# Two layers written out without a loop, with the splits of weights laid between tiles and row parts

## The reference

```python
for i in range(2):
    x = x + 0.5 * swiglu_ffn(rmsnorm_2(x, ffn1_norm[i]), ffn1_wi[i], ffn1_wo[i])
    u = rmsnorm_2(x, mix_norm[i])
    mq, mk, mv, mo, mi, mf, sq, sk, sv, ga, gb = jnp.split(u @ w_in[i], offsets, axis=-1)
    hA = rmsnorm_2(mlstm_chunkwise(mq, mk, mv, mi + b_igate[i], mf + b_fgate[i]), ml_out_norm[i])
    yA = (jax.nn.sigmoid(mo) * hA) @ w_a[i]
    hB = swa_sink_attention(sq, sk, sv, q_norm[i], k_norm[i], sinks[i], rel_bias)
    mixed = jax.nn.sigmoid(ga) * yA + jax.nn.sigmoid(gb) * (hB @ w_b[i])
    x = x + mixed @ w_out[i]
    x = x + 0.5 * swiglu_ffn(rmsnorm_2(x, ffn2_norm[i]), ffn2_wi[i], ffn2_wo[i])
    gate = jax.nn.sigmoid(rmsnorm_2(x, ple_norm[i]) @ w_ple_gate[i])
    x = x + gate * (p[i] @ w_ple[i])
```

## Time and profile before

| | us |
|---|---|
| median of three runs | 2400.02 |
| the profiled execution's own time | 2400.93 |
| its span | 2398.9 |
| TensorE matmul busy | 1921.8 (80%) |
| TensorE weight load busy | 1366.8 (57%) |
| VectorE busy | 969.2 (40%) |
| ScalarE busy | 696.0 (29%) |
| GpSimd busy | 40.6 (2%) |

### The profile page before, as it was taken

One profiled execution on the slowest core, in us unless ns is written; L12 is line 12 of the kernel. 1 busy time (PEld: TensorE's weight loads), 2 busy tenths in 40 slices (PEclk: granted clock), 3 DMA queues, 4 the chain that ended last, 5 costly groups with the idle time before them and its releaser, 6 DMA issues.

```text
span 2398.9 us, 34233 instructions
## 1 busy us (share of the span) xinstructions
PE 1921.8 (80%) x12667; PEld 1366.8 (57%) x12667; DVE 969.2 (40%) x1348; ACT 696.0 (29%) x963; POOL 40.6 (2%) x68
## 2 busy tenths in 40 slices
PE   6996655655555555565899999899989999989998
PEld 4774111211111111111799877799879988778997
DVE  3474000000000000000676576666656666666665
ACT  4331000000000000000444455444444444544443
POOL 0000000000000000000000000000000000000000
PEclk9997778778787778778999999999999999999999
DMA  9767999999999999999556553355535565344561
GB/s 370 251 241 331 429 428 429 428 428 429 428 428 428 428 428 428 428 428 410 181 199 217 163 157 123 122 176 196 189 107 182 186 203 176 124 136 150 171 208 55
DMA packets 174825, 660.85 MB, mean 275 GB/s; under 512 B 10053, under 2 KB 108142, under 8 KB 143734
## 3 DMA queue, kind: packets, MB, share of 16 engines
q1 hardware_dynamic: 171980, 654.12, 70.4%
q10 hardware_dynamic: 2376, 3.03, 0.6%
q0 software_dynamic: 352, 2.11, 0.2%
HBM read 656.60 MB, written 2.64 MB: 275 GB/s over the span
## 4 chain that ended last, share of the span: by engine, by line
issue 77%; PE 17%; DVE 3%; ACT 1%; POOL 1%; DMA 1%; POOLq 0%; ACTq 0%; DVEq 0%; PEldq 0%; PEld 0%
PE PS L1862 12%; PE PS L1577 2%; DVE units L205 1%; DVE arena L205 1%; DMA ring<-in_w_ada 1%; PE PS L1546 1%; ACT units L205 0%; POOL arena L604 0%; PE PS L1643 0%; PE PS L1661 0%; DVE hn L205 0%; POOLq L603 0%; POOLq L629 0%; DVE x L205 0%; DVE hT_split L205 0%
## 5 line engine op out<-in xcount | busy, mean ns | idle before, releaser
L205 DVE TENSOR_TENSOR units<-ring,units 128x1024 fp32r<-128x1024 f32 (+2 forms) x416 | 505.7, 1216 | 206.7 <-ACT units L205 172.1
L205 ACT ACTIVATE units<-ring 128x1024 fp32r<-128x1024 f32 (+2 forms) x416 | 438.0, 1053 | 482.7 <-PE PS L1862 447.4
L1862 PE MATMUL PS<-hT_split,units 128*128 128x256 f32 x4416 | 554.9, 286 | 10.0 <-DVE hT_split L205 8.4
L1862 PEld LDWEIGHTS PS<-hT_split,units 128*128 128x128 f32 x4416 | 547.8, 194 | 20.5 <-DVE hT_split L205 11.3
L205 DVE SCALAR_TENSOR_TENSOR arena<-arena,PS 128x512 f32<-128x512 f32 (+1 forms) x54 | 41.4, 767 | 802.5 <-ACT arena L205 513.1
L205 ACT ACTIVATE arena<-PS 32x256 f32<-32x256 f32 (+4 forms) x135 | 66.8, 495 | 945.9 <-PE PS L1832 310.7
L1862 PE MATMUL PS<-units,hT_split 128*128 128x512 f32 (+2 forms) x1248 | 294.2, 396 | 13.3 <-DVE hT_split L205 9.0
L1862 PEld LDWEIGHTS PS<-units,hT_split 128*128 128x128 f32 x1248 | 238.1, 195 | 61.3 <-DVE hT_split L205 9.8
L1862 PE MATMUL PS<-units,hid_split 128*128 128x512 f32 x1056 | 255.6, 392 | 0.0
L1862 PEld LDWEIGHTS PS<-units,hid_split 128*128 128x128 f32 x1056 | 192.8, 189 | 37.0 <-issue 0.9
L1824 PE MATMUL PS<-moe_ring,arena 128*32 128x512 f32 x768 | 124.5, 781 | 98.9 <-DMA moe_ring<-in_w_gate_e 55.8
(11 more groups left out here) (208 smaller groups left out, 1254.7 us busy)
## 6 DMA issues: line engine op xcount, KB each, us to landing
ring<-in_ffn_wi SPq DMA_DIRECT2D x88, 1024.0 KB, 5.4
ring<-in_w_gate_e SPq DMA_DIRECT2D x24, 2048.0 KB, 36.0
moe_ring<-in_w_up_e SPq DMA_DIRECT2D x24, 2048.0 KB, 36.4
ring<-in_w_down_e SPq DMA_DIRECT2D x24, 2048.0 KB, 35.6
moe_ring<-in_w_gate_e SPq DMA_DIRECT2D x24, 2048.0 KB, 36.7
ring<-in_w_up_e SPq DMA_DIRECT2D x24, 2048.0 KB, 36.5
moe_ring<-in_w_down_e SPq DMA_DIRECT2D x24, 2048.0 KB, 36.2
ring<-in_ffn_wo SPq DMA_DIRECT2D x44, 1024.0 KB, 4.9
```

The costliest lines, as they stand in the source:

```text
L205: return instruction(*args, **kwargs)
L1862: passes = [mm(out, lhs[i], rhs[j], start=start and i + j == 0, stop=stop and i == 1, **flags) for i, j in ((0, 0), (0, 1), (1, 0))]
```

## The change

The layer loops of all engines become Python loops: each engine's program holds both layers, and semaphore targets outside the FFN loops are constants. The FFN loops stay. The first units of layer 1's FFN1 are split inside layer 0's PLE stage, and the first square of `x` is taken there. Unit rests are laid between token tiles and between row parts. The first product of an FFN takes both its units part by part (`first_up`). The transposed parts of the mix stage lie in other banks, so that half of `ple_up` can go ahead of them. Squares and sums of queries and keys go ahead of the scans. ScalarE makes `a_split` ahead of `sw_exp(7)`.

```diff
-def turned_bank(name):
-    return 0 if name in ("mix", "ple") else 4
+def turned_bank(name, k):
+    return {"mix": (0, 1, 4, 5), "ple": (0, 1, 2, 3)}.get(name, (4, 5, 6, 7))[k % 4]
+ROOT_BANK = {"ffn1": 3, "mix": 0, "ffn2": 3}
...
-            with sp.Fori(0, LAYERS) as l:
+            for l in range(LAYERS):
...
-            for l in act.loop(LAYERS):
+            for l in range(LAYERS):
                 before = FIRST_UNITS + l * LAYER_UNITS
                 layer_fills = l * (LAYER_SLOTS // R * 16)
-                gate_up_hi(OFF_FFN1, 0, before, layer_fills)
+                if l == 0:
+                    gate_up_hi(OFF_FFN1, 0, before, layer_fills)
...
                     sw_copy(h)
+                    if h == 6:
+                        halves_hi(stage_units(OFF_WA, 2, 0, 2), D, before, layer_fills)
+                        act.wait_ge(S["branch_T"], 2 * l + 1)
+                        activation(a_split[:, 0, :, :].rearrange("p k n -> p (k n)"), two_banks(4), ACT.Copy).then_inc(
+                            S["branch_hi"], 1)
                     if h + 1 < SW_H:
                         sw_exp(h + 1)
...
                     if h == 6:
-                        halves_hi(stage_units(OFF_WA, 2, 0, 2), D, before, layer_fills)
-                        act.wait_ge(S["branch_T"], 2 * l + 1)
-                        activation(a_split[:, 0, :, :].rearrange("p k n -> p (k n)"), two_banks(4), ACT.Copy).then_inc(
-                            S["branch_hi"], 1)
                         act.wait_ge(S["sink_arg"], l + 1)
...
+                        if l + 1 < LAYERS:
+                            gate_up_hi(OFF_FFN1, 0, before + LAYER_UNITS, layer_fills + LAYER_SLOTS // R * 16)
+                            square_of(0, "x_layer", (NT * (l + 1) + 1,))
                         act.wait_ge(S["unit_used"], before + LAYER_UNITS)
...
-            for l in dve.loop(LAYERS):
+            for l in range(LAYERS):
                 before = FIRST_UNITS + l * LAYER_UNITS
-                split_rest(2 * OFF_FFN1, gate_up_weights(POS_LAYER + OFF_FFN1, 0, 0), before)
+                if l == 0:
+                    gate_up_rest(OFF_FFN1, 0, before)
                 dve.wait_ge(S["gain_full"], (l + 1) * 16)
                 norm_T_rest("ffn1", l)
-                split_rest(2 * OFF_FFN1 + 1, gate_up_weights(POS_LAYER + OFF_FFN1, 0, 1), before)
...
-                piece_rest(0, 0, 2)
+                piece_rest(0, 0, 1)
                 dve.wait_ge(S["row_roots"], scaled_turn("ffn1", l))
                 add_rows("ffn1", by_root, "x_ffn1", l, OFF_Z)
-                piece_rest(0, 2)
-                norm_T_rest("mix", l)
+                for u in range(4):
+                    if u > 0:
+                        piece_rest(0, u, u + 1)
+                    norm_T_rest("mix", l, (2 * u, 2 * u + 1))
...
                 sw_scores(0)
+                piece_rest(5, 2)
                 sw_scores(1)
...
-                halves_rest(stage_units(OFF_WA, 2, 0, 2), D, before)
                 dve.wait_ge(S["branch_hi"], 2 * l + 1)
                 tt(a_split[:, 1, :, :].rearrange("p k n -> p (k n)"), PS[:, 4:6, :].rearrange("p b n -> p (b n)"),
...
-                halves_rest(stage_units(OFF_WA, 2, 2), D, before)
+                halves_rest(stage_units(OFF_WA, 2), D, before)
...
+                    if t == 0:
+                        halves_rest(stage_units(OFF_WO, 4, 0, 2), D, before)
+                norm_T_rest("mixed", l, range(3))
+                halves_rest(stage_units(OFF_WO, 4, 2, 3), D, before)
+                norm_T_rest("mixed", l, range(3, 5))
+                halves_rest(stage_units(OFF_WO, 4, 3, 4), D, before)
+                norm_T_rest("mixed", l, range(5, KT))
+                halves_rest(stage_units(OFF_WO, 4, 4), D, before)
+                add_rows("mixed", lambda t: 0.5, "x_mix", l, OFF_FFN2, lambda: gate_up_rest(OFF_FFN2, 0, before))
...
-                halves_rest(stage_units(OFF_PLE, 4, 2, 4), D, before)
-                norm_T_rest("ple", l)
+                norm_T_rest("ple", l, range(2))
+                for u in range(1, 4):
+                    halves_rest(stage_units(OFF_PLE, 4, u, u + 1), D, before)
+                    norm_T_rest("ple", l, range(2 * u, 2 * u + 2))
...
+                if l + 1 < LAYERS:
+                    gate_up_rest(OFF_FFN1, 0, before + LAYER_UNITS)
...
+                    def first_up(base, turn):
+                        pe.wait_ge(S["unit_split"], base + 2 * off + 2)
+                        for k in range(KT):
+                            pe.wait_ge(S["hT"], KT * turn + (k + 1))
+                            for part in range(2):
+                                _, last = split_mm(PS[:, 0, part * TOK:(part + 1) * TOK],
+                                                   [unit(i, 2 * off + part, KT, P)[:, k, :] for i in range(2)],
+                                                   [hT_split[:, i, k, :] for i in range(2)],
...
-                transpose_rows("mix", x, "x_ffn1", l, 0)
...
+                ple_up(0, 0, 2)
+                transpose_rows("mix", x, "x_ffn1", l)
+                ple_up(0, 1, 3)
```

More of the change, by code:

```diff
@@ L1272, in ffn_hidden, with add_rows @@
                     sub(c, hidden, base)
-            def add_rows(name, scale, signal, l, off):
+            def add_rows(name, scale, signal, l, off, between=None):
                 bank = 0 if name == "mixed" else 4
@@ L1280, in add_rows @@
                     else:
+                        if between is not None:
+                            between()
                         dve.wait_ge(S["unit_used"], FIRST_UNITS + l * LAYER_UNITS + 2 * off)
@@ L1344, in _ @@
                 dve.run(V.reduce_sum, qk_ms[:, 16:20], tmp_k, AX.X).then_inc(S["ms_qk"], 1)
-                piece_rest(4, 2)
+                piece_rest(4, 0, 2)
+                dve.wait_ge(S["f_ln"], l + 1)
+                tt(G(5), G(2), G(4), ALU.subtract)
+                dve.run(V.tensor_tensor_scan, G(6), G(5), zeros[0:ML_H, :], 0.0, ALU.add, ALU.add)
+                dve.wait_ge(S["z_copied"], 3 * l + 3)
+                tt(G(7), G(0), G(6), ALU.subtract)
+                dve.run(V.tensor_tensor_scan, G(1), G(7), G(7), 0.0, ALU.max, ALU.max)
+                tt(G(2), G(6), G(1), ALU.add).then_inc(S["scan"], 1)
+                dve.wait_ge(S["qk_roots"], l + 1)
+                tt(by16(sq), by16(sq), wide_of(qk_ms[:, 0:16], DH), ALU.mult)
+                tt(by16(sk), by16(sk), wide_of(qk_ms[:, 16:20], DH), ALU.mult)
+                piece_rest(4, 2)
+                kd_v = kd.rearrange("p t (g u d) -> p (t g) u d", g=SW_KV, u=2)
+                for u in range(2):
+                    tt(kd_v[:, :, u, :], by16(sk), p_("k_gain").unsqueeze(1).to_broadcast([P, 4, DH]), ALU.mult)
+                tt(by16(sq), by16(sq), p_("q_gain").unsqueeze(1).to_broadcast([P, 16, DH]),
+                   ALU.mult).then_inc(S["qk_normed"], 1)
                 used_to(OFF_Z + 8)
@@ L1855, in _ @@
                     last.then_inc(S["combined" if t == 1 else "combined_first"], 1)
-            with pe.Fori(0, LAYERS) as l:
+            for l in range(LAYERS):
                 layer_fills = l * (LAYER_SLOTS // R * 16)
@@ L1923, in ffn, with up @@
                 def ffn(off, hidden, base, turn, name):
-                    def up(c, base, turn=None):
+                    def first_up(base, turn):
[6 more added lines that the diff above has]
+                                                   [hT_split[:, i, k, :] for i in range(2)],
+                                                   start=(k + part == 0), stop=(k == KT - 1), skip_group_check=True)
+                                if k == KT - 1:
+                                    last.then_inc(S["unit_used"], 1)
+                    def up(c, base):
                         for part in range(2):
@@ L1929, in up @@
                             for k in range(KT):
-                                if turn is not None and part == 0:
-                                    pe.wait_ge(S["hT"], KT * turn + (k + 1))
                                 first, last = split_mm(PS[:, c % 4, part * TOK:(part + 1) * TOK],
@@ L1955, in down @@
                         last.then_inc(S["unit_used"], 1)
-                    up(0, base, turn)
+                    first_up(base, turn)
                     row_of_roots(name, l)
```

78 lines of the change are left out of this document (29 added, 49 removed).

## The result

The kernel after takes 2342.72 us, the median of four runs (2341.2 to 2343.59), against 2399.43 before in the same series: a ratio of 0.9765, 95% interval 0.9751 to 0.9779. That is 56.7 us less where 50 were forecast; the range held it. The profiled execution took 2341.2 us, its span is 2339.2, so the two spans differ by 59.7.

What follows compares the result with a forecast made beforehand. In the layers TensorE was the bound, with 43.6 us of waits on VectorE and half speed behind them. Terms summed to 52.2, giving 2347.8 from 2400.02; with one or two slow pieces left, 2350 us, range 2338 to 2368.

Steps and rivals of the forecast that it cites:

- the second halves of the forecast's terms: At the places in the layers, the share of each gain from products returning to full speed, beside the idle time removed.
- The branch: Branch in both layers: of idle 3.43 us some 3.2 go, 24 products fall from 8.48 to 5.73; 10.4 for both.
- FFN2: Entry of FFN2: idle 2.29 us loses 1.8, 48 products fall from 8.57 to 6.02; 8.7 for both layers.
- layer 1's entry: Start of layer 1: idle 3.81 us shrinks to about 0.2, 48 products fall from 9.06 to 6.02; 6.6 once.
- the query norm: Sums ahead of scans: 0.9 of idle 1.80 us and all of 2.09 go, 1.6 more in layer 1; 7.6.
- The mix entry: Half the PLE product goes ahead of the transposes: 1.7 and 0.7 us in layer 0, 1.5 in layer 1; 3.9.
- The PLE entry: Entry of the PLE stage: idle 2.29 us loses 1.8, 96 products fall from 24.94 to 22.36; 8.8 for both layers.
- Layer 0's entry: Start of layer 0: bounds of 1.4 us lost by a second unit rest and 1.2 gained by interleaved products; taken as 0.
- The mixed entry: Products with `w_out`: idle 2.23 us falls to about 0.4, 96 products fall from 23.68 to 22.36; 6.2 for both layers.
- The half speed stays: Rival, places in the layers: pauses shrink but products behind stay slow; 20.7 us given back, 2370; chance 0.18.
- The wait behind `qk_roots`: Rival at the query norm: late unit rests starve TensorE inside piece 4, the 7.6 us gain goes, 2365; chance 0.08.
- The third rival: FFN loops: unrolling shifts their bodies, 16 back edges cost more, 2428 us at 7 more each; chance 0.04, half slower.

Runs made afterwards that it cites:

- old_branch: The kernel after with the unit copies, `a_split` and its rest put back behind the exponential and the units at the branch; 2351.37 us, ratio 0.9798.
- old_query_norm: The kernel after with the scans ahead of the sums again and the order of pieces 4 and 5 undone; 2352.80 us, ratio 0.9809.
- unroll_two: The kernel before with only the layer loops of ScalarE and VectorE written out; 2383.90 us, ratio 0.9938.

## Why the prediction was right

**The bound.** Right. TensorE's waits on VectorE and the half speed behind them were what could be had: TensorE is busy for 26.1 us less, against some 24 in the second halves of the forecast's terms (2.6 + 5.1 + 5.2 + 5.5 + 1.6 + 0.7 + 3.0), the rest idle time.

**The places.** The branch (10.2 for 10.4), FFN2 (8.7 for 8.7), layer 1's entry (6.7 for 6.6) and the query norm (7.9 for 7.6) came as worked out, and `old_branch` and `old_query_norm` return theirs when undone. The idle on `units` was forecast at 1 and is 1.09; the units 2 and 3 of `w_a` came late by 0.57 for 0.8.

**The step that was wrong** is "Constants in place of registers shorten steps of VectorE that lie beside TensorE's work [...] Both cost nothing". At the entries VectorE's steps are just what TensorE waits for, as the first part of the same text says; there 0.07 us for a part and 0.08 for a unit are on the path. With the loop's end, the only part that had been booked, unrolling alone is worth 16 us, four times that. The sum still came out near, because the terms overlap: unrolling 15.6 (`unroll_two`), the interleaving 17.3, the query norm 10.1, the branch 8.7, `first_up` 6.5 and splitting ahead 2.1 make 60.3 without the mix entry. A piece at half speed that goes by unrolling can't go again by the order. That the terms worked out from the kernel before held this well is helped by this overlap, which the text did not reckon with. Had I booked the unrolling on top of the places, I would have forecast some 62 us.

**Terms of the wrong size.** The mix entry gave 6.1 for 3.9. In layer 0 the forecast said 2.4; from the start of the idle time to piece 0 it was 8.5 us and is 4.8: the first half of `ple_up` overruns by 0.3 (0.45 counted), the transposes take 1.8 from start to start where they took 3.1 (0.7 counted), and from there to the piece it is 1.3 (1.85 counted). The PLE entry gave 2.2 more: one unit fewer ahead of `add_rows` also took the idle 1.2 ahead of its transposes, in both layers, which the text had overlooked. Layer 0's entry, between 1.4 lost and 1.2 gained, gave 2.0: outside the bounds, though by a piece at full speed that another execution of the same code did not have. The mixed entry gave 0.9 less, by layer 1's piece at half speed, one of the "one or two" that were let stand; the other is the one at 1411.14. They cost 1.6 each, for 1.7.

**The rivals.** "The half speed stays" fell: with the pauses, the products behind them came back to full speed, but for layer 1's mixed entry. The wait behind `qk_roots` is real and costs 1.09 and 0.97, not 2 and a slow piece. The FFN turns did not grow. The third rival's premise was wrong: the 2.8 us at a turn's start, taken for the price of the back edge, are the wait for the `down` product, and stand there without a loop too. What a back edge costs VectorE lies hidden in that wait, if it costs anything.

What stays open is why, at nearly equal pauses, one place is slow behind it and another not. The mix entry was not undone by itself, so its 6.1 is read from the traces alone.

## What to carry to other kernels

Read the engine that the bottleneck waits for as if it were the bottleneck, for the length of that wait: there its loop registers, its gaps of a tenth and its loop's end all count; where TensorE did not wait for VectorE, none of them was seen. Lay what is not needed at once (the splits of weights) into that engine's own waits, so that nothing stands between an input's arrival and its first use. Don't add up gains that remove the same pause; measure one part alone and one part undone before saying which of them earned it. And before an idle time is called a loop's price, read the target of the wait that ends it.

## What the runs showed of the hardware

**Half speed is not fixed by the pause in front.** At the PLE entry the 96 products took 24.94 behind 2.29 us, and 22.02 behind 2.13. At layer 1's mixed entry they took 23.66 behind pauses of 1.72 and 0.34, while layer 0's, behind 1.87 and 0.34, took 22.05. And a slow piece came behind no pause at all, only small matmuls, at 1411.14 in the kernel after; window 1413:1415 there and 2092:2094 in layer 1:

```profile
1413.00:1415.00 2.00, 2.00 (x7) 1.51 (x6) 1.72 (x4) 1.92 (x2) 0.00 (x0) 0.50 0.00 0
2092.00:2094.00 2.00, 2.00 (x7) 1.51 (x6) 1.82 (x3) 1.18 (x4) 0.00 (x0) 0.50 0.00 0
```

PEclk is 0.50 in both, 1.2 GHz. The clearest case is layer 0's entry, shown with the result: the same program behind the same pauses took 5.99 us in one execution and 8.65 in another. The Trainium skill (TensorE: Matmul & The Clock Gate, Part 1, "A second HAM failure mode: psum-queue depth-cycling") describes a clock that swings when TensorE stands still for moments, but often. The piece at 1411.14 does not look like that in the profile: from 1399 to 1411 TensorE is busy for 12.00 of 12.00 us at a granted clock of 1.00, and no run here tested it.

**A loop costs by the engine.** On VectorE steps in the loop stood 0.17 us apart where the same steps with constants stand 0.1 apart, and the end of the layer loop, with its drain, cost some 3.4 us. On TensorE neither was seen (ratio 1.0005).
